# Exchanging rotation halves from POOL's queue instead of SyncE's, in a two-block model on one core

## The chip, the core and the metric

The kernel runs on one core of a Trainium2 chip. The core has TensorE (PE, matrix products), VectorE (DVE), ScalarE (ACT), GpSimd (POOL) and SyncE (SP), which here does nothing but issue transfers, and 16 DMA engines that carry them. Each engine works through its own instructions in order, and semaphores tie the engines to each other. The metric is the device time of one execution in microseconds. Lower is better.

## What is computed

256 tokens of width 1024 pass through two layers of a first block and one layer of a second. A layer of the first block projects the normalised input with one wide matrix and feeds three branches: a gated memory (mLSTM), a gated linear recurrence (RG-LRU) and a sparse attention, whose indexer keeps 64 keys for each query. A gated sum, an output projection and a feed-forward part follow. The second block has a state-space branch, a short convolution and a mixture of experts. The change touches only the rotary embedding of the attention's query, key and indexer projections:

```python
def apply_rope(x, cos, sin):
    x1, x2 = jnp.split(x.astype(jnp.float32), 2, axis=-1)
    c = cos[:, :, None, :]
    s = sin[:, :, None, :]
    return jnp.concatenate([x1 * c - x2 * s, x2 * c + x1 * s], axis=-1).astype(x.dtype)
...
        q_c = apply_rope(a_q.reshape(a_shape), cos, sin)
        k_c = apply_rope(a_k.reshape(a_shape), cos, sin)
        qi = apply_rope(a_qi.reshape(B, S, IDX_HEADS, IDX_DIM), cos, sin)
        ki = apply_rope(a_ki[:, :, None, :], cos, sin)[:, :, 0, :]
        y_c = dsa_attention(q_c, k_c, a_v.reshape(a_shape), qi, ki, a_w).reshape(B, S, D_BRANCH)
```

## The kernel before

All programs are written out by hand, one for each engine, with an explicit wait before each instruction that needs one. Features lie on partitions and tokens along the free dimension. A layer of the first block streams weight chunks of 1 MB through three slots. SP loads chunk c into `w_raw`. ACT rounds it to `w_hi` (`split`, L744), and DVE subtracts to get `w_lo` (L1256). PE then makes three products for each pair of tiles (L2118 to L2120). SP may load chunk c when the `w_lo` of chunk c - 3 is done. After each chunk every engine runs its `side(L, c)`: the small work that is placed beside the chunks.

Chunks 4 to 9 are the projections that get rotated: two each for the indexer's queries (`qi`), the queries and the keys. Call these tiles, and their pairs of buffers, 0 to 5. A tile holds two blocks of 128 features (four heads of 64) for 256 tokens:
- ACT copies PE's result out of the bank into `rope_in[n % 2]` (L804). From the third tile on it first waits until the buffer's cosine product (`rope_cos`) and exchange (`rope_swap`) are done.
- The rotation needs the upper 32 rows of a head in the place of the lower 32, and the other way round. Engines work along partitions, so transfers inside the on-chip memory do that: `swap_pair` issues four for a tile, each of 32 partitions by 512 numbers (64 KB), into `rope_sin[i % 2]`. `swap_key` issues two for the single key of the indexer. From tile 2 on `swap_pair` waits for `rope_done`, since the buffer it writes must have been used up.
- POOL multiplies `rope_in` by the cosines (L702), once for each tile.
- DVE multiplies `rope_sin` by the sines (L1356), waits for the cosine product, and adds (L1360): `rope(L, i)`. After tile 0 it rotates the indexer's key as well (L1365 to L1369).

PE computes indexer scores from `qi` and `ki` after chunks 8, 9 and 10 (L2252). The first needs three rotations: tiles 0 and 1 and the key. ACT applies the relu to them (L941), DVE sums (L1412) and selects the keys (L1428, L1430). The attention logits follow on DVE (L1454) with the row maximum (L1460), the exponential and the normalisation on ACT (L838, L849), and on PE the transposes of the probabilities after chunk 17 (L2263).

SP's part of a layer is one list. The exchanges stand in it between loads: the key's and tile 0's just ahead of load 10, tile i's ahead of load 10 + i. POOL has little to do: six cosine products, eight sums of the merge (L710), and some set-up.

Of the kernel before, what the change touches and what calls it, by code (L numbers as in the profile page):

```python
# [56 lines left out]
RING = 3  # L57
# [95 lines left out]


MERGE = max(WB)


SWAP_AT = 4 + 2 * RING

# [43 lines left out]
def program(nc, xT, positions, par_1, consts, w_in, w_a, w_x, w_branch, w_out, ffn_up, ffn_down,  # L206
            par_2, mask_2, metaT, w_in_2, w_out_2, w_group, w_expert, e_gate, e_up, e_down, out):
    ctx = ExitStack()
    with ctx:
# [221 lines left out]
        def need(eng, name, L, k):  # L431

            v = L * COUNT[name] + k
            if not isinstance(v, int) or v > 0:
                eng.wait_ge(sem[name], v)
# [83 lines left out]
        def _(sp):  # L519
# [84 lines left out]
                sp.dma_start(raw_m[i % RAWS].rearrange("p (t c) -> p t c", t=2), src)\  # L604
                    .then_inc(sem[moe_landed(i)], 16)

            def swap_halves(dst, src, first_rows, name):

                for r in first_rows:
                    sp.dma_start(dst[r:r + 32], src[r + 32:r + 64]).then_inc(sem[name], 16)  # L610
                    sp.dma_start(dst[r + 32:r + 64], src[r:r + 32]).then_inc(sem[name], 16)

            def swap_key(L):
                need(sp, "rows_ready", L, 1)
                swap_halves(ki_sin, rope_ki, (64,), "ki_swap")

            def swap_pair(L, i):

                need(sp, "evac_act", L, 2 + i + 1)
                if i >= 2:  # L620
                    need(sp, "rope_done", L, i if i > 2 else 1)
                swap_halves(rope_sin[i % 2], rope_in[i % 2], (0, 64), f"rope_swap{i % 2}")

            def layer(L, next_source):

                load(L, 2, source(L, 2))
                sp.wait_ge(sem["zeros_ready"], 1)
                load_small(L)
                for c in range(RING, MIX):
                    if c == SWAP_AT:  # L630
                        swap_key(L)
                    if SWAP_AT <= c < SWAP_AT + 6:
                        swap_pair(L, c - SWAP_AT)
                    load(L, c, source(L, c))
                load(L, MIX, ffn_source(L, 0, 0))
                load(L, MIX + 1, ffn_source(L, 1, 0))
                if L == DEPTH - 1:

                    need(sp, "y_lo", L, 5)
                    for dst, src in ((p2[:], par_2), (mask2[:], mask_2),  # L640
                                     (meta[:], metaT.rearrange("(k p) t -> p k t", p=P)),
                                     (w_route[:, :, 0:4], w_group[0].rearrange("(k p) n -> p k n", p=P)),
                                     (w_route[:, :, 4:20], w_expert[0].rearrange("(k p) n -> p k n", p=P)),
                                     (dt_w[:], w_in_2[0][:, COL_2["dt"]:COL_2["dt"] + HEADS_S]
                                      .rearrange("(k p) n -> p k n", p=P))):
                        sp.dma_start(dst, src).then_inc(sem["par_2"], 16)
                    for upper, j in ((0, 0), (0, 1), (1, 0), (1, 1)):
                        sp.dma_start(nff_m[64 * upper:64 * upper + 64, j::2],
                                     par_2[j::2, Q_NFF + upper:Q_NFF + KT:2],
                                     allow_slow_non_contiguous=True).then_inc(sem["par_2"], 16)  # L650
                with sp.Fori(0, N_FF - 1) as n:
                    load(L, MIX + 2, ffn_source(L, 0, n + 1), n)
                    load(L, MIX + 3, ffn_source(L, 1, n + 1), n)
                    load(L, MIX + 4, ffn_source(L, 2, n), n)
                load(L, PER_LAYER - 1, ffn_source(L, 2, N_FF - 1))
                load(L, PER_LAYER, next_source(0))
                load(L, PER_LAYER + 1, next_source(1))
# [24 lines left out]
        @block.gpsimd  # L682
        def _(pool):
            own = Own(pool, "own_pool")
            own(nc.gpsimd.memset(wa[:], 0.0))
            own(nc.gpsimd.memset(wx[:], 0.0))
            own(nc.gpsimd.memset(small_raw, 0.0))
            own(nc.gpsimd.memset(eps[:], EPS))
            own.settle()
            nc.gpsimd.memset(ones[:], 1.0).then_inc(sem["zeros_ready"], 1)  # L690

            def layer(L):

                for c in range(MIX - 1):
                    if 4 <= c <= 9:

                        i = c - 4
                        dst = (qi, q_c, k_c)[i // 2][:, 2 * (i % 2):2 * (i % 2) + 2, :]
                        need(pool, "evac_act", L, 2 + i + 1)
                        if i == 0:  # L700
                            need(pool, "act_lo", L, 4)
                        nc.gpsimd.tensor_tensor(dst, rope_in[i % 2], cos_t[:].unsqueeze(1).to_broadcast([P, 2, T]),  # L702
                                                ALU.mult).then_inc(sem["rope_cos"], 1)
                    if c in WB[2:]:

                        for half in range(2):
                            i = 2 * WB[2:].index(c) + half
                            b = 2 * (i % 4)
                            need(pool, "evac_dve", L, evacuations(c, True) + half + 1)
                            nc.gpsimd.tensor_tensor(merged[:, b:b + 2, :], merged[:, b:b + 2, :], merge_t[half],  # L710
                                                    ALU.add).then_inc(sem["wb_sum"], 1)

            pool.wait_ge(sem["setup_act"], 2)
            for L in range(DEPTH):
                layer(L)


            pool.wait_ge(sem["par_2"], 160)
            pool.wait_ge(sem["x_ready"], DEPTH * 8)
            nc.gpsimd.tensor_copy(hx[:, :, 0:META], meta[:]).then_inc(sem["meta_ready"], 1)  # L720
            nc.gpsimd.tensor_tensor(w_route[:], w_route[:], p2[:, Q_NFF:Q_NFF + KT].unsqueeze(2)
                                    .to_broadcast([P, KT, 20]), ALU.mult).then_inc(sem["moe_consts"], 1)

            mixed_out(pool)
            nc.gpsimd.tensor_scalar(diag[:], ident[0:20, 0:20], p2[0:20, Q_RB:Q_RB + 1], None, ALU.mult)\
                .then_inc(sem["moe_consts"], 1)
            nc.gpsimd.tensor_scalar(tri[:], cst[:, K_CAUS:K_CAUS + P], 0.0, None, ALU.is_equal)\
                .then_inc(sem["moe_consts"], 1)
            nc.gpsimd.iota(first_of[:], [[P, PER_GROUP]], base=0, channel_multiplier=0,
                           allow_small_or_imprecise_dtypes=True).then_inc(sem["moe_consts"], 1)  # L730
            nc.gpsimd.iota(place[:], [[1, SLOTS]], base=0, channel_multiplier=0,
                           allow_small_or_imprecise_dtypes=True).then_inc(sem["moe_consts"], 1)
# [2045 lines left out]
```

## Time and profile before

| | |
|---|---|
| median of 3 runs | 1684.63 us (1683.84 to 1685.64) |
| the profiled execution's own time | 1684.37 us |
| its span | 1682.4 us |
| PE busy | 1586.4 us, 94% |
| DVE busy | 1283.9 us, 76% |
| ACT busy | 946.7 us, 56% |
| POOL busy | 49.1 us, 3%, in 43 instructions |
| transfers | 325.89 MB |

The busy shares are means over a long program. The exchanges take place in two short stretches, from about 58 to 108 us in the first layer and from about 571 to 622 us in the second. The time of the profiled execution is 2.0 us longer than its span: what lies around the program. Every transfer of the kernel is issued on SP's queue, and the row of an issue tells how long SP was held by it, not how long the data took.

### The profile page before, as it was taken

The page shows a single profiled execution, that of the slowest core. Times are in us where ns is not written, and L with a number is a line of the kernel's source. Part 1 is how long each engine was busy: PE and PEld are TensorE (multiplying, and loading weights), DVE is VectorE, ACT ScalarE, POOL GpSimd, SP SyncE. Part 2 cuts the span into 40 slices and gives each one's busy share as a digit, 9 for nine tenths or more (in the row PEclk, how much of TensorE's full clock was granted, in tenths as well). Part 3 has the DMA queues.
Part 4 walks back from the last instruction along what each step waited for, and adds up shares of the span by engine and source line. Part 5 has one row for each costly group of instructions (what it writes and reads, how often), then busy time and mean ns, then how long its engine had stood idle before and what let it go on. Part 6 is the DMA issues. An engine that isn't in the chain of part 4 may idle for free.

```text
span 1682.4 us, 27823 instructions
## 1 busy us (share of the span) xinstructions
PE 1586.4 (94%) x11504; PEld 1486.7 (88%) x11504; DVE 1283.9 (76%) x1573; ACT 946.7 (56%) x1012; POOL 49.1 (3%) x43
## 2 busy tenths in 40 slices
PE   3999999999997999999999998799999899999998
PEld 3989999999997989999999997698899688888886
DVE  6798685776676798776676667885895788888986
ACT  4747655554444747655554444555643667777674
POOL 0110001000000010001000000000000000000000
PEclk9999999999998999999999999899999899999999
DMA  7455445455555465545555555254344499999993
GB/s 208 141 175 171 149 132 176 151 200 177 184 177 149 134 194 156 158 125 170 169 199 176 178 185 161 76 161 140 101 153 150 157 346 365 365 350 359 355 359 115
DMA packets 223262, 325.89 MB, mean 194 GB/s; under 512 B 21568, under 2 KB 180032, under 8 KB 223168
## 3 DMA queue, kind: packets, MB, share of 16 engines
q1 hardware_dynamic: 223168, 324.55, 58.4%
q8 instruction: 70, 1.15, 0.3%
q14 instruction: 24, 0.20, 0.0%
HBM read 320.20 MB, written 1.05 MB: 191 GB/s over the span
## 4 chain that ended last, share of the span: by engine, by line
PE 78%; DVE 13%; ACT 5%; issue 3%; DMA 1%; POOL 0%; SPq 0%; DVEq 0%; ACTq 0%
PE bank L2118 24%; PE bank L2120 23%; PE bank L2119 23%; DVE w_lo L1256 2%; ACT w_hi L744 1%; DMA w_raw<-in_w_in 1%; PE bank L2452 1%; DVE w_lo L1707 1%; DVE work L1736 1%; PE bank L2558 1%; DVE work L1250 1%; DVE work L1356 1%; PE bank L2611 0%; DVE work L1412 0%; ACT work L838 0%
## 5 line engine op out<-in xcount | busy, mean ns | idle before, releaser
L1256 DVE TENSOR_TENSOR w_lo<-w_raw,w_hi 128x2048 fp32r<-128x2048 f32 x158 | 362.8, 2296 | 121.3 <-ACT w_hi L744 120.6
L2118 PE MATMUL bank<-act_h,w_hi 128*128 128x256 f32 (+1 forms) x1408 | 406.4, 289 | 21.0 <-DVE act_l L1292 9.5
L2119 PE MATMUL bank<-act_l,w_hi 128*128 128x256 f32 (+1 forms) x1408 | 398.9, 283 | 0.0
L2120 PE MATMUL bank<-act_h,w_lo 128*128 128x256 f32 (+1 forms) x1408 | 398.9, 283 | 0.0
L744 ACT CAST w_hi<-w_raw 128x2048 fp32r<-128x2048 f32 x158 | 300.6, 1902 | 42.4 <-PE bank L2120 34.2
L2118 PEld LDWEIGHTS bank<-act_h,w_hi 128*128 128x128 f32 x1408 | 268.0, 190 | 28.0 <-issue 23.0
L2119 PEld LDWEIGHTS bank<-act_l,w_hi 128*128 128x128 f32 x1408 | 268.1, 190 | 0.4
L2120 PEld LDWEIGHTS bank<-act_h,w_lo 128*128 128x128 f32 x1408 | 267.9, 190 | 0.0
L2118 PE MATMUL bank<-u_h,w_hi 128*128 128x256 f32 x768 | 217.5, 283 | 0.0
L2120 PE MATMUL bank<-u_h,w_lo 128*128 128x256 f32 x768 | 217.2, 283 | 0.0
L2119 PE MATMUL bank<-u_l,w_hi 128*128 128x256 f32 x768 | 215.3, 280 | 0.0
L2118 PE MATMUL bank<-y_h,w_hi 128*128 128x256 f32 x704 | 200.0, 284 | 3.0 <-DVE y_l L1618 3.0
L2120 PE MATMUL bank<-y_h,w_lo 128*128 128x256 f32 x704 | 198.4, 282 | 0.0
L2119 PE MATMUL bank<-y_l,w_hi 128*128 128x256 f32 x704 | 197.5, 280 | 0.0
L2119 PEld LDWEIGHTS bank<-u_l,w_hi 128*128 128x128 f32 x768 | 146.0, 190 | 0.1
L2118 PEld LDWEIGHTS bank<-u_h,w_hi 128*128 128x128 f32 x768 | 144.1, 188 | 0.1
L2120 PEld LDWEIGHTS bank<-u_h,w_lo 128*128 128x128 f32 x768 | 143.7, 187 | 0.0
L2118 PEld LDWEIGHTS bank<-y_h,w_hi 128*128 128x128 f32 x704 | 132.2, 188 | 3.6 <-issue 3.4
L2119 PEld LDWEIGHTS bank<-y_l,w_hi 128*128 128x128 f32 x704 | 133.2, 189 | 0.2
L2120 PEld LDWEIGHTS bank<-y_h,w_lo 128*128 128x128 f32 x704 | 132.0, 188 | 0.0
L1912 DVE TENSOR_TENSOR w_lo<-w_raw,w_hi 128x2048 fp32r<-128x2048 f32 x52 | 118.8, 2289 | 13.9 <-ACT w_hi L1133 13.0
L1133 ACT CAST w_hi<-w_raw 128x2048 fp32r<-128x2048 f32 x52 | 99.3, 1912 | 36.4 <-PE bank L2120 36.4
(467 smaller groups left out, 2845.6 us busy)
## 6 DMA issues: line engine op xcount, KB each, us to landing
w_raw<-in_w_in SPq DMA_DIRECT2D x88, 1024.0 KB, 5.5
w_raw<-in_ffn_up SPq DMA_DIRECT2D x48, 1024.0 KB, 5.2
w_raw<-in_e_gate SPq DMA_DIRECT2D x25, 1024.0 KB, 7.3
w_raw<-in_ffn_down SPq DMA_DIRECT2D x24, 1024.0 KB, 4.9
w_raw<-in_e_up SPq DMA_DIRECT2D x22, 1024.0 KB, 7.1
w_raw<-in_e_down SPq DMA_DIRECT2D x22, 1024.0 KB, 7.2
w_raw<-in_w_out SPq DMA_DIRECT2D x16, 1024.0 KB, 5.0
w_raw<-in_w_branch SPq DMA_DIRECT2D x12, 1024.0 KB, 5.1
```

The source lines that it names most:

```text
L744: nc.scalar.copy(w_hi[c % RING][:], w_raw[c % RING][:]).then_inc(sem["hi_ready"], 1)
L1133: nc.scalar.copy(hi_m[i % SPLITS], raw_m[i % RAWS]).then_inc(sem["hi_ready"], 1)
L1250: step(STT(t_c, t_c, 1.0 / k, t_b, ALU.add, ALU.mult))
L1256: V.tensor_tensor(w_lo[c % RING][:], w_raw[c % RING][:], w_hi[c % RING][:].bitcast(F32), ALU.subtract).then_inc(sem[f"lo_ready{c % RING}"], 1)
L1356: own(V.tensor_tensor(rope_sin[i % 2], rope_sin[i % 2], sin_t[:].unsqueeze(1).to_broadcast([P, 2, T]), ALU.mult))
L1707: V.tensor_tensor(w_lo[c % RING][:], w_raw[c % RING][:], w_hi[c % RING][:].bitcast(F32), ALU.subtract).then_inc(sem[f"lo_ready{c % RING}"], 1)
L1736: ins = STT(dst[:, j, s:TM], psum[(2 * c + half) % 4][:, 0:TM - s], p2[:, col:col + 1], dst[:, j, s:TM], ALU.mult, ALU.add)
L1912: V.tensor_tensor(lo_m[h], raw_m[i % RAWS], hi_m[h].bitcast(F32), ALU.subtract)\
L2118: mm(out, a_hi, b_hi, start=first, stop=False, skip_group_check=True)
L2119: mm(out, a_hi, b_lo, start=False, stop=False, skip_group_check=True)
L2120: return mm(out, a_lo, b_hi, start=False, stop=last, skip_group_check=True)
L2452: ins = mm(psum[6 + g % 2][r:r + 64, o + t_0:o + T], xdt[0:rows, s, h * 64:h * 64 + 64], weight[h % 2][0:rows, col:col + n], start=s == 0, ...
```

## The change

The functions `swap_halves`, `swap_key` and `swap_pair` move from the program of SP to that of POOL, with their waits. POOL calls `swap_pair(L, i)` right ahead of the cosine product of tile i, and `swap_key(L)` ahead of that for tile 0. SP keeps its loads, and the constant that placed the exchanges among them goes. The buffers, the semaphores and the transfers themselves stay as they are.

```diff
-SWAP_AT = 4 + 2 * RING
...
                 for c in range(RING, MIX):
-                    if c == SWAP_AT:
-                        swap_key(L)
-                    if SWAP_AT <= c < SWAP_AT + 6:
-                        swap_pair(L, c - SWAP_AT)
                     load(L, c, source(L, c))
...
+            def swap_halves(dst, src, first_rows, name):
+
+                for r in first_rows:
+                    nc.gpsimd.dma_start(dst[r:r + 32], src[r + 32:r + 64]).then_inc(sem[name], 16)
+                    nc.gpsimd.dma_start(dst[r + 32:r + 64], src[r:r + 32]).then_inc(sem[name], 16)
+
+            def swap_key(L):
+                need(pool, "rows_ready", L, 1)
+                swap_halves(ki_sin, rope_ki, (64,), "ki_swap")
+
+            def swap_pair(L, i):
+
+                need(pool, "evac_act", L, 2 + i + 1)
+                if i >= 2:
+                    need(pool, "rope_done", L, i if i > 2 else 1)
+                swap_halves(rope_sin[i % 2], rope_in[i % 2], (0, 64), f"rope_swap{i % 2}")
+
...
                         i = c - 4
+                        if i == 0:
+                            swap_key(L)
+                        swap_pair(L, i)
                         dst = (qi, q_c, k_c)[i // 2][:, 2 * (i % 2):2 * (i % 2) + 2, :]
                         need(pool, "evac_act", L, 2 + i + 1)
```

POOL's queue before, from the end of the set-up through the first layer's merge (L702 is the cosine product, the ISA ahead of it POOL's configuration, L710 the merge; `work` is the tensor that holds `rope_in`, `rope_sin` and the rotated tiles):

```order
L690 MEMSET ones 128x256 [waits own_pool]
L702 ISA
L702 TENSOR_TENSOR work<-work,cos_t 128x512 [waits act_lo,evac_act,setup_act]
L702 TENSOR_TENSOR work<-work,cos_t 128x512 [waits evac_act] x5
L710 TENSOR_TENSOR work<-work 128x512 [waits evac_dve] x8
```

The same place in the changed kernel, after the two issues for the indexer's key: tiles 0 and 1 whole, and the first transfer of tile 2 (lines 670 and 671 are the two issues in `swap_halves`, L697 is the cosine product):

```order
L670 DMA work<-work 32x512 [waits evac_act]
L671 DMA work<-work 32x512
L670 DMA work<-work 32x512
L671 DMA work<-work 32x512
L697 ISA
L697 TENSOR_TENSOR work<-work,cos_t 128x512 [waits act_lo,evac_act]
L670 DMA work<-work 32x512 [waits evac_act]
L671 DMA work<-work 32x512
L670 DMA work<-work 32x512
L671 DMA work<-work 32x512
L697 TENSOR_TENSOR work<-work,cos_t 128x512 [waits evac_act]
L670 DMA work<-work 32x512 [waits rope_done,evac_act]
```

Each cosine product stands behind four issues now, from the third tile on behind a wait for `rope_done` as well, and the configuration stands behind the first six issues.

SP's queue before, from the load of chunk 10 to tile 2's first transfer (L555 is a load, L610 and L611 are the exchanges):

```order
L555 DMA w_raw1<-in_w_in 128x8x256 [waits lo_ready1]
L610 DMA work<-work 32x512 [waits evac_act]
L611 DMA work<-work 32x512
L610 DMA work<-work 32x512
L611 DMA work<-work 32x512
L555 DMA w_raw2<-in_w_in 128x8x256 [waits lo_ready2]
L610 DMA work<-work 32x512 [waits rope_done,evac_act]
```

and from the load of chunk 9 in the changed kernel (L551 is the load):

```order
L551 DMA w_raw0<-in_w_in 128x8x256 [waits lo_ready0]
L551 DMA w_raw1<-in_w_in 128x8x256 [waits lo_ready1]
L551 DMA w_raw2<-in_w_in 128x8x256 [waits lo_ready2]
L551 DMA w_raw0<-in_w_in 128x8x256 [waits lo_ready0]
L551 DMA w_raw1<-in_w_in 128x8x256 [waits lo_ready1]
```

SP's loads follow each other with nothing but their own waits between them.

## Rows read from the trace of the kernel before

**Rows 1.** Waits of PE: who waited for whom, us in total, times, longest.

```profile
PE bank L2263 <- ACT work L849: 5.5, 2, 3.3
...
PE bank L2252 <- ACT work_b L941: 4.3, 2, 2.1
...
PE bank L2252 <- DVE work L1360: 2.8, 2, 1.4
```

**Rows 2.** Chain of waits, first layer: start us, us, engine and line.

```profile
56.92 0.47 ACT work L906
...
137.51 2.30 DVE tiny L1460
...
155.17 1.62 PE bank L2263 x8
```

**Rows 3.** Stretches: from:to, length, then busy us (instructions) of PE, PEld, DVE, ACT, POOL.

```profile
64.40:142.20 77.80, 74.28 (x608) 71.71 (x607) 75.43 (x119) 42.12 (x52) 11.59 (x6) 0.98 0.54 156
142.20:155.20 13.00, 9.72 (x84) 9.52 (x82) 8.94 (x29) 12.96 (x24) 0.00 (x0) 1.00 0.53 163
```

**Rows 4.** L702's summary (ns min/median/max), then timeline of POOL: start us, us, instruction.

```profile
L702 POOL TENSOR_TENSOR work<-work,cos_t x12: 1307/1632/3216, 66.8 to 611.2; 128x512 f32<-128x512 f32 x12
L702 POOLq MODIFY_POOL_CONFIG  x2: 11/11/11, 3.0 to 3.0; - x2
...
66.75 1.31 POOL L702 TENSOR_TENSOR work<-work,cos_t 128x512 f32<-128x512 f32 x1 [63.75 <-ACT work L804]
73.40 2.33 POOL L702 TENSOR_TENSOR work<-work,cos_t 128x512 f32<-128x512 f32 x1 [5.34 <-ACT work L804]
...
90.30 3.22 POOL L702 TENSOR_TENSOR work<-work,cos_t 128x512 f32<-128x512 f32 x1 [5.19 <-ACT work L804]
```

**Rows 5.** Timeline of DVE, first layer.

```profile
66.46 0.41 DVE L1246 TENSOR_TENSOR work<-work 4x256 f32<-4x256 f32 x1
66.91 1.43 DVE L1247 TENSOR_TENSOR work<-work 4x256 f32<-4x256 f32 x1
...
83.24 0.69 DVE L1360 TENSOR_TENSOR work<-work 128x512 f32<-128x512 f32 x1
...
86.22 0.29 DVE L1369 COPY work<-work 64x256 f32<-64x256 f32 x1
...
88.75 0.68 DVE L1356 TENSOR_TENSOR work<-work,sin_t 128x512 f32<-128x512 f32 x1
...
90.08 2.29 DVE L1256 TENSOR_TENSOR w_lo<-w_raw,w_hi 128x2048 fp32r<-128x2048 f32 x1
92.28 1.79 DVE L1356 TENSOR_TENSOR work<-work,sin_t 128x512 f32<-128x512 f32 x1
94.10 0.69 DVE L1360 TENSOR_TENSOR work<-work 128x512 f32<-128x512 f32 x1
...
102.71 0.68 DVE L1356 TENSOR_TENSOR work<-work,sin_t 128x512 f32<-128x512 f32 x1
...
108.60 0.69 DVE L1356 TENSOR_TENSOR work<-work,sin_t 128x512 f32<-128x512 f32 x1
...
114.22 0.69 DVE L1356 TENSOR_TENSOR work<-work,sin_t 128x512 f32<-128x512 f32 x1
```

**Rows 6.** Issues of L610 (ns min/median/max), their landing, and SP's waits, 57 to 115.

```profile
L610 SPq DMA_DIRECT2D work<-work x26: 507/590/607, 59.2 to 618.7; - x26
...
DMA to landing us min/median/max: 2.0/4.1/5.4
...
SPq L555 <- DVE w_lo L1256: 30.5, 7, 5.5
```

**Rows 7.** Timeline of ACT, first layer; in brackets its idle time before and who ended it.

```profile
77.81 0.57 ACT L804 COPY work<-bank 128x512 f32<-128x512 f32 x1
...
89.64 0.58 ACT L804 COPY work<-bank 128x512 f32<-128x512 f32 x1 [4.26 <-DMA work<-work]
...
140.04 0.51 ACT L838 ACTIVATE work<-work,tiny 128x256 f32<-128x256 f32 x1 [0.95 <-DVE tiny L1461]
```

More of the change, by code:

```diff
@@ L605, in load_moe @@
                     .then_inc(sem[moe_landed(i)], 16)
[L607 to L622, printed above, removed]
             def layer(L, next_source):
```

## Prediction

> **What bounds the kernel now.** I read first who waits on TensorE, since PE is busy for 94% of the span. Near the exchanges it waits three times in each of the two layers: 1.4 us for a rotation (DVE, L1360), 2.1 us for a relu (ACT, L941), and 2.2 to 3.3 us, some 50 us later, for the softmax's normalisation (ACT, L849) [rows 1]. Then I read the chain of waits through the first layer. From 56.9 us it runs on ACT and then on DVE, passes the rotations, reaches the row maximum at 137.5 and comes back to PE only at 155.2, with the transposes of the probabilities [rows 2]. So what PE loses at 90 and at 106 us is not paid by the end. Without those two stalls it would stand before the transposes that much earlier, and wait there that much longer. What counts is DVE's work in that stretch. The stretch view says how full DVE is: busy 75.43 of 77.80 us, with nearly all the rest in gaps of hundredths between dependent instructions [rows 3]. After it ACT is busy for 12.96 of 13.00 us. The second layer repeats the first 513 us later.
>
> The second thing to see is what POOL's cosine product costs DVE. It runs six times a layer, 1.31 us at the least [rows 4]. The first starts at 66.75, and the 4x256 product L1247 that DVE begins under it takes 1.43 us, where the same form just before took 0.41: 1.0 us lost. The fifth starts at 90.30, under a w_lo subtraction that runs to 92.4, and is stretched to 3.22 us. DVE's next product, L1356, then takes 1.79 us where it elsewhere takes 0.68: 1.1 us lost [rows 4, 5]. So a cosine product costs DVE about 1.0 us wherever both have two-input work, and it waits for the DVE instruction that was there first.
>
> **What is removed: SP's issues.** SP issues 52 exchanges, 26 a layer, at 0.59 us [rows 6]. They hold up no weight load: of the seven loads between 57 and 115 us each is released by a w_lo subtraction of DVE, for which SP waits 30.5 us in all. So a freer SP issues no load earlier. The other gain would be faster landing, since on SP an exchange stands behind a 1 MB load and lands in a median of 4.1 us. It is late only once: the fifth evacuation on ACT waits 4.26 us for a transfer and runs at 89.64, after PE had finished that chunk [rows 7]. Neither PE nor DVE waits for that evacuation. Gain: 0.
>
> **What is added: 52 issues on POOL.** No row shows a transfer issued by POOL. Call the time that one holds POOL d. From below the nearest row is SP's shortest issue, 0.51 us; from above, POOL held until the transfer lands, 4.1 us [rows 6]. Between these lie SP's usual issue (0.59) and POOL's own instruction on a tile of this size (1.31). I take d = 1.0, between the last two. The Trainium skill, "DMA: Bandwidth & Descriptors", table on latency, gives about 1 us to the first byte for a transfer issued by GpSimd and 0.6 for one by SP; taken as an estimate of d, it gives the same sum.
>
> **What is moved: each cosine product goes behind its pair's four issues, and behind their wait for rope_done.** This is the step to follow closely. POOL's order is four issues (4d), the cosine (1.5 us, between the shortest, 1.31, and the median, 1.63 [rows 4]), then the next pair. Pairs 0 and 1 start when ACT has evacuated their tiles, 0.1 us before their cosines of now (66.75 and 73.40). Pairs 2 to 5 can't begin until an earlier rotation on DVE is done: pair 2 after rotation 0 (83.9), pair 3 after rotation 1 (90.2), pair 4 after rotation 2 (94.8), pair 5 after rotation 3 (104.1). DVE wants pair i for rotation i, at 82.5 (the L1356 just before L1360), 88.75, 92.28, 102.71, 108.60 and 114.22 [rows 5]. With d = 1.0, and 2 us from the last issue to landing (the fastest landing on SP), the first layer becomes:
> pair 0: from 66.6, cosine ends 72.1, landed 72.6, wanted 82.5
> pair 1: from 73.4, cosine ends 78.9, landed 79.4, wanted 88.75
> pair 2: from 83.9, cosine ends 89.4, landed 89.9, wanted 92.28
> pair 3: from 90.2, cosine ends 95.7, landed 96.2, wanted 102.71
> pair 4: from 95.7, cosine ends 101.2, landed 101.7, wanted 108.60
> pair 5: from 104.1, cosine ends 109.6, landed 110.1, wanted 114.22
> Nothing is late; the closest is pair 2, with 2.4 us to spare. Landing at SP's median of 4.1 us instead would bring pair 2 to 92.0, still in time. The evacuation at 89.64 moves to about 89.9. For which d does the cover end? Pair 2 is late when 83.9 + 4d + 2 passes 92.28, at d = 1.6; the queue as a whole when pairs 2 to 5 follow each other without a break, 83.9 + 4(4d + 1.5) + 0.5 = 114.2, at d = 1.5. So up to 1.5 us the issues are hidden behind DVE.
>
> **Collisions.** The six cosines move by 4 to 11 us, but all still fall between 70 and 110 us, where DVE's work is two-input almost throughout. So 6 x 1.0 us are lost as before: change 0, and perhaps one more or one less. What differs is the order. By the end of rotation 1 three cosines have met DVE and not four, so PE's 1.4 us stall should shrink; as said, that is handed on to the wait at the transposes.
>
> **A program step that moves too.** The order shows POOL's configuration instruction (ISA) just ahead of the first cosine, now behind the first six issues, while before it was over at 3.0 us, long before it was needed; its own row has 11 ns [rows 4]. If its effect has a latency, the first cosine pays it. The first layer has 82.5 - 72.1 = 10 us of room there, and the evacuation at 77.81, which needs the first cosine, 5.7 us [rows 7]. Cost 0. The Trainium skill, "GPSIMD Engine Reference", section 2 (Architecture), says that the first call of freshly loaded code pays about 6 us; by that the first cosine would end at 78.1, and pair 1 at about 84, still ahead of rotation 1 at 88.75.
>
> **The sum.** Profiled execution 1684.37 us (its span 1682.4 and 2.0 around it), median of the runs 1684.63. SP's relief 0, hidden issues 0, collisions 0 (plus or minus 1.0 a layer), and 0.4 us a layer for a few small slips (the evacuation, an interfering DVE instruction): 1684.6 + 0.8 = **1685.4 us**. About 0.2%, 3.4 us, is what a measurement of this kernel can tell from no change.
>
> **Rivals.** *POOL becomes the bound of the rotations (slower).* The mechanism is d over 1.5. At d = 2.0 pair 0 ends at 76.1, pair 1 at 85.6, and pair 2, begun at once, at 95.1 with the landing at 95.6, so rotation 2 is 3.3 us late. Pair 4 lands at 114.6, against rotation 4 at 111.9: 2.7 more. Pair 5 lands at 124.1, against 120.2: 3.9 more. That is 9.9 us a layer on a full DVE, 1704 us. At 1.75 it is about half, 1694. For it: six queue steps in series with nothing in them idle. Against it: SP does the same for 0.59, and the room per pair is 2 to 8 us. At the far end, 4.1, a pair takes 17.9 us and six of them end near 174, some 60 us a layer late: 1804. Chance 0.2.
> *Descriptors and DVE get in each other's way (slower).* The rows show POOL and DVE excluding each other in two-input work. If POOL's issues also hold up DVE's copies and scalar operations, two of these a layer fall under them (the copy at 86.22 [rows 5] is one), up to one d each: 4 x 1.0 = 4 us, 1688.6. The Trainium skill, "SBUF — State Buffer", section "SBUF: two separate sides", has this rule, as the "DVE blocks DMA" trap: a transfer issued by GpSimd needs the port pair that VectorE takes for its fast copies, and which started first blocks the other; no row here has such a transfer. Chance 0.08.
> *DVE gets free (faster).* A cosine that lands on DVE's one-input or idle time costs nothing, and PE's stalls fall by 1.4 + 2.1 us. For it: 1.0 us for each cosine is real. Against: DVE is full to 142, and ACT was idle only 1.0 us before the row maximum reached it [rows 7], so an earlier DVE gains at most that until ACT binds. To pass 3.4 us both layers must gain 1.7, which takes a lower ACT cost too. 1684.6 - 2 x 1.9 = 1681. Chance 0.12.
> *The issues on POOL cost what they do on SP (no change).* With 0.59 us the pairs are ready 1.6 us sooner each, and no one waits for them: 1684.6. This lies within the forecast.
>
> **Chances.** Forecast, with that last case, 0.6; POOL bound 0.2; port 0.08; faster 0.12. The range leaves out d above about 1.8 (0.13) and gains over 3.6 us (0.06): 1681 to 1696. Faster 0.12; within 0.2% 0.62 (forecast, and a part of the port case); slower 0.26.
>
> **What would show it.** Right: POOL transfers of about 1 us, no idle time of DVE before L1356, six cosines a layer at the places above, the 1.4 us wait of PE for L1360 gone or smaller, and PE's wait for L849 longer by as much. Wrong: DVE waiting at L1356 for a transfer (d or the landing too long), its total over 64 to 142 us changed by more than 2 us (collisions), or POOL idle between its issues for long (it is the landing or the configuration, not d).

## The result, and the profile after

| | before | after |
|---|---|---|
| median of 6 runs each | 1684.82 us (1683.84 to 1686.12) | 1692.1 us (1689.82 to 1692.77) |
| profiled execution, its span | 1684.37, 1682.4 | 1692.77, 1690.7 |
| DVE busy | 1283.9 us | 1287.6 us |
| POOL busy | 49.1 us, 43 instructions | 71.0 us, 95 instructions |

The changed kernel takes 1.004 times the time of before, with a 95% interval of 1.003 to 1.005: 7.3 us slower. That is more than the 3.4 us that a measurement can tell from no change. A second set of five runs gave 1.0037 [1.0024, 1.005]. The range held the time, but the forecast was "no change", and what came is the slower side. Three executions that were far off (one of experiment 7 at 3921.8 us, two of the kernel before at 1767.0 and 8376.86) are left out of every figure. Code lines after the change are five lower than before: L1356 is now L1351, L1360 is L1355, L1256 is L1251, L849 is L844, L941 is L936.

POOL's issues first. The summaries of the first of the two issue lines, of its landing and of the cosine (ns min/median/max), and then POOL's timeline of the first layer (start us, us, instruction), to be read against [rows 4, 6]:

```profile
L670 POOL DMA_DIRECT2D work<-work x26: 496/500/727, 59.2 to 622.2; - x26
...
DMA to landing us min/median/max: 1.8/2.4/5.2
L697 POOL TENSOR_TENSOR work<-work,cos_t x12: 1277/1316/2392, 69.3 to 623.2; 128x512 f32<-128x512 f32 x12
L697 POOLq MODIFY_POOL_CONFIG  x2: 37/37/37, 69.2 to 69.2; - x2
```

```profile
68.70 0.50 POOL L671 DMA_DIRECT2D work<-work  x1
69.30 1.32 POOL L697 TENSOR_TENSOR work<-work,cos_t 128x512 f32<-128x512 f32 x1
...
92.28 0.50 POOL L671 DMA_DIRECT2D work<-work  x1
92.79 1.32 POOL L697 TENSOR_TENSOR work<-work,cos_t 128x512 f32<-128x512 f32 x1
...
107.25 0.50 POOL L671 DMA_DIRECT2D work<-work  x1
107.76 1.28 POOL L697 TENSOR_TENSOR work<-work,cos_t 128x512 f32<-128x512 f32 x1
```

An issue holds POOL for 0.50 us, half of what the sum assumed and less than the 0.59 on SP. It lands in a median of 2.4 us instead of 4.1. By every number on which the schedule rested, the change did better than forecast.

DVE's timeline of the first layer, to be read against [rows 5]:

```profile
68.02 4.67 DVE L1245 SCALAR_TENSOR_TENSOR work<-work 4x256 f32<-4x256 f32 x7
...
76.51 1.52 DVE L1378 SCALAR_TENSOR_TENSOR work<-work 4x256 f32<-4x256 f32 x1
...
82.49 0.67 DVE L1351 TENSOR_TENSOR work<-work,sin_t 128x512 f32<-128x512 f32 x1
...
87.71 1.79 DVE L1351 TENSOR_TENSOR work<-work,sin_t 128x512 f32<-128x512 f32 x1
...
92.34 2.32 DVE L1351 TENSOR_TENSOR work<-work,sin_t 128x512 f32<-128x512 f32 x1
...
96.56 3.83 DVE L1539 TENSOR_TENSOR_SCAN work<-work 128x256 f32<-128x256 f32 x4
...
107.46 3.73 DVE L1251 TENSOR_TENSOR w_lo<-w_raw,w_hi 128x2048 fp32r<-128x2048 f32 x1
```

No idle time stands before any L1351: nothing is late. But look at the durations. L1351 takes 2.32 us at 92.34, against 0.67 at 82.49. The `w_lo` subtraction takes 3.73 at 107.46, against 2.29. One instruction in each of the six places is longer than its form is elsewhere, by 1.57, 1.10, 1.11, 1.64, 1.39 and 1.44 us: 8.2 us for six cosines. The six of before cost 0.9 to 1.1 each and 6.1 together. Two of the six have kept that price: their cosines waited for a DVE instruction that was there first (their rows last 1.79 and 2.39 us where the others last 1.3). The other four cost 1.4 to 1.6 us. And L1351 at 92.34 begins while POOL is still issuing, 0.45 us before the cosine's shown start.

The stretch view (length, then busy us of PE, PEld, DVE, ACT, POOL; clock, DMA share, GB/s), against [rows 3]:

```profile
64.70:144.70 80.00, 75.94 (x621) 73.47 (x621) 77.61 (x119) 42.13 (x52) 21.45 (x30) 0.98 0.52 152
144.70:157.70 13.00, 8.16 (x70) 7.95 (x69) 8.94 (x29) 12.96 (x24) 0.00 (x0) 0.97 0.53 161
```

DVE does the same 119 instructions in 77.61 us instead of 75.43, and the stretch is 2.2 us longer. ACT's part behind it is as it was. From here on I measure "DVE's stretch" from the start of the reciprocal (L1245 before) to the start of the row maximum (L1460 before), in both layers, where DVE stands idle for hundredths only: 72.82 and 72.87 us before, 74.98 and 74.62 after. That is 3.9 us of the 8.3 between the spans.

PE's waits and its granted clock show where more went. PE's waits of after (us in total, times, longest), against [rows 1], and then the windows behind the second layer's transposes of the probabilities, after and before, each with its columns as above:

```profile
PE bank L2258 <- ACT work L844: 9.8, 2, 4.9
...
PE bank L2247 <- ACT work_b L936: 6.1, 2, 3.1
...
PE bank L2247 <- DVE work L1355: 1.8, 2, 1.1
```

```profile
673.00:676.00 3.00, 2.85 (x14) 2.85 (x15) 2.75 (x17) 3.00 (x5) 0.00 (x0) 0.50 0.22 35
676.00:679.00 3.00, 3.00 (x16) 3.00 (x16) 2.82 (x12) 0.74 (x2) 0.00 (x0) 0.50 0.81 314
679.00:683.00 4.00, 4.00 (x35) 4.00 (x35) 3.05 (x3) 0.28 (x1) 0.00 (x0) 0.97 0.00 0
```

```profile
668.00:671.00 3.00, 2.44 (x21) 2.44 (x22) 2.81 (x13) 3.00 (x5) 0.00 (x0) 1.00 0.09 10
671.00:675.00 4.00, 4.00 (x36) 4.00 (x35) 3.76 (x16) 1.17 (x3) 0.00 (x0) 1.00 0.66 255
```

After the change PE works at the lower level (0.50 of full speed, 1.2 GHz) for 6 us behind its 4.9 us wait, 16 matmuls in 3 us. Before, the wait was 2.2 us and the clock stayed at the full 2.4 GHz. PE's timeline gives the price: from these transposes to the next group of them it takes 6.59 us before (668.56 to 675.15) and 9.37 after (673.15 to 682.52).

```profile
668.56 1.09 PE L2263 MATMUL bank<-cst,work 128*128 128x128 f32 x8 [2.22 <-ACT work L849]
```

```profile
673.15 1.97 PE L2258 MATMUL bank<-cst,work 128*128 128x128 f32 x8 [4.91 <-ACT work L844]
```

So the 8.3 us between the two spans are, in order of time: 0.34 ahead of the first stretch, 2.16 in it, 0.36 up to the second, 1.75 in it, 2.78 of clock behind it, and 0.9 in the rest. The three small ones (1.6 us together) have no cause that I found.

### The profile page after: what moved, and what is told of

Its sections match the earlier page's. It is cut to its first block, busy times and chain, and to the rows that moved or that the text cites. A ratio compares the mean times of both kernels' runs of the same rounds, so it can differ in the third digit from the quotient of the medians.

```text
span 1690.7 us, 27824 instructions
## 1 busy us (share of the span) xinstructions
PE 1589.4 (94%) x11504; PEld 1489.9 (88%) x11504; DVE 1287.6 (76%) x1573; ACT 946.9 (56%) x1012; POOL 71.0 (4%) x95
## 3 DMA queue, kind: packets, MB, share of 16 engines
HBM read 320.20 MB, written 1.05 MB: 190 GB/s over the span
## 4 chain that ended last, share of the span: by engine, by line
PE 76%; DVE 15%; ACT 4%; issue 3%; DMA 1%; POOL 0%; SPq 0%; DVEq 0%; ACTq 0%
PE bank L2113 23%; PE bank L2115 23%; PE bank L2114 23%; DVE w_lo L1251 3%; ACT w_hi L739 1%; DVE work L1407 1%; DVE work L1351 1%; PE bank L2447 1%; DMA w_raw<-in_w_in 1%; DVE work L1245 1%; DVE w_lo L1702 1%; PE bank L2553 1%; DVE work L1731 1%; PE bank L2606 0%; DVE work L1539 0%
## 5 line engine op out<-in xcount | busy, mean ns | idle before, releaser
L1251 DVE TENSOR_TENSOR w_lo<-w_raw,w_hi 128x2048 fp32r<-128x2048 f32 x158 | 365.6, 2314 | 122.4 <-ACT w_hi L739 121.6
```

The costliest lines, as they stand in the source:

```text
L1251: V.tensor_tensor(w_lo[c % RING][:], w_raw[c % RING][:], w_hi[c % RING][:].bitcast(F32), ALU.subtract).then_inc(sem[f"lo_ready{c % RING}"], 1)
```

## The experiments

The first question was why a cosine product costs DVE more. Theory A: it is a lock. POOL's cosine reads two operands, and DVE's two-input work needs the same interface. The cosine now follows an issue with no wait of its own that is still open, and takes the interface while POOL is still busy issuing. Theory B: it is position. The cosines start at other moments, and meet longer DVE instructions. Theory C: POOL's transfers themselves disturb DVE. Each ratio is to runs of the kernel before that were taken together with the experiment: their median is 1685.6 us for experiments 1, 2, 4 and 5, 1684.33 for 3, 6, 7 and 8, and 1685.77 for 9.

### 1. The cosine product ahead of the issues

```diff
                         i = c - 4
-                        if i == 0:
-                            swap_key(L)
-                        swap_pair(L, i)
...
                         nc.gpsimd.tensor_tensor(dst, rope_in[i % 2], cos_t[:].unsqueeze(1).to_broadcast([P, 2, T]),
                                                 ALU.mult).then_inc(sem["rope_cos"], 1)
+                        if i == 0:
+                            swap_key(L)
+                        swap_pair(L, i)
```

> POOL issues the exchanges, but each cosine product stands ahead of its pair's four issues and not behind them. Lock theory (a cosine product that follows an issue with no wait of its own holds DVE off already during the last issue, so that DVE loses 1.4 to 1.65 us where it lost 1.0): here each cosine product is released by a semaphore again, the six cost DVE about 1.0 us each as before the change (6.1 us a layer, not 8.3), time 1685 +- 1. Rival (POOL's issues themselves hold up DVE): the loss stays, time 1690 or more.

Measured: 1687.67 us, ratio 1.001 [1.0001, 1.0018], between what I expected (1685) and the rival's 1690. DVE's stretch is 73.55 and 73.62 us: 0.7 more than before, where the changed kernel has 2.16 and 1.75 more. It is only half a test, as the timeline of POOL shows: three cosines come after idle time, and the later three, shown here, stand right behind the issues of the previous tile.

```profile
87.79 2.38 POOL L694 TENSOR_TENSOR work<-work,cos_t 128x512 f32<-128x512 f32 x1
94.01 1.31 POOL L694 TENSOR_TENSOR work<-work,cos_t 128x512 f32<-128x512 f32 x1
99.19 1.53 POOL L694 TENSOR_TENSOR work<-work,cos_t 128x512 f32<-128x512 f32 x1
```

```profile
93.56 2.32 DVE L1351 TENSOR_TENSOR work<-work,sin_t 128x512 f32<-128x512 f32 x1
```

One of the three, that of 94.01, finds a DVE instruction that began 0.45 us before it, and that one loses 1.6 us. The others cost 0.9 to 1.1.

### 2. The cosine waits until its own exchange has landed

```diff
                             need(pool, "act_lo", L, 4)
+                        need(pool, f"rope_swap{i % 2}", L, 64 * (i // 2 + 1))
                         nc.gpsimd.tensor_tensor(dst, rope_in[i % 2], ...
```

> The changed kernel, with one wait more: POOL's cosine product waits until its pair's exchange has landed, so it still stands behind the issues, and later than in the changed kernel, but it is released by a semaphore. Lock theory: 1.0 to 1.1 us of DVE for each cosine product, DVE's total back to that of before, time 1685 to 1687, more only if ACT's evacuations come late by the 2 us that the cosine waits longer. Position rival (what costs is that the cosines meet other DVE instructions now): 1690 or more, since the positions stay late. Issue rival (POOL's issues disturb DVE): 1690 or more as well.

Measured: 1685.68 us, ratio 1.0001 [0.9992, 1.0011]. One wait, which makes POOL do its work later, removes all but 0.2 us of the loss in a stretch. DVE's stretch is 72.96 and 73.09, and DVE is busy for 1284.0 us, as before. POOL's and DVE's timelines at one place:

```profile
85.31 0.50 POOL L671 DMA_DIRECT2D work<-work  x1
87.67 1.29 POOL L698 TENSOR_TENSOR work<-work,cos_t 128x512 f32<-128x512 f32 x1 [1.87 <-DMA work<-work]
```

```profile
67.98 3.09 DVE L1246 SCALAR_TENSOR_TENSOR work<-work 4x256 f32<-4x256 f32 x7
...
86.97 0.69 DVE L1352 TENSOR_TENSOR work<-work,sin_t 128x512 f32<-128x512 f32 x1
87.69 1.82 DVE L1356 TENSOR_TENSOR work<-work 128x512 f32<-128x512 f32 x1
```

L1356 begins with the cosine and loses 1.1 us, the price of before; L1352, ahead of it, is untouched. So are the seven L1246, which end at 71.07, across the start of the first cosine at 70.70: 3.09 us, where after the change they took 4.67. This speaks for A and against C, since the issues are all still there. B is not out yet: the cosines have moved too.

### 3. The kernel before, with that same wait

SP issues the exchanges as before; only the wait of experiment 2 is added on POOL. It moves the cosines of the first layer to 72.35, 83.99, 89.58, 95.68, 100.32 and 109.85, each with its idle time ahead.

> The kernel before, with SP issuing, where POOL's cosine product waits until its pair's exchange has landed. So the cosine products move to about the places of the changed kernel, but nothing is issued by POOL and each is released by a semaphore. Lock theory: 1.0 to 1.1 us each, as before, time 1685 to 1686. Position rival: slower, 1688 or more, since the cosine products meet other DVE instructions.

Measured: 1686.1 us, ratio 1.0006 [0.9998, 1.0015], DVE's stretch 72.91 and 73.12. Six other positions, and each still costs 1.0 to 1.1 us. With that theory B falls: a cosine that was released from an open wait costs the same at every place tried.

### 4. Cosine products on DVE, exchanges on SP

```diff
-        rope_in = [at(4, 2, T), at(6, 2, T)]
+        rope_in = [at(4, 2, T), at(6, 2, T), at(57, 2, T), at(59, 2, T), at(61, 2, T), at(63, 2, T)]
...
+                own(V.tensor_tensor(dst, rope_in[i], cos_t[:].unsqueeze(1).to_broadcast([P, 2, T]), ALU.mult))
                 own(V.tensor_tensor(rope_sin[i % 2], rope_sin[i % 2],
...
-                need(dve, "rope_cos", L, i + 1)
```

POOL's cosine product is gone, and the DVE products stand in `rope(L, i)`. Each tile has its own `rope_in`, so ACT no longer waits for a buffer, only for the last rotation before it writes `mv` there.

> The kernel before, with the six cosine products on DVE instead of POOL, and six buffers for the evacuated tiles so that ACT need not wait for them. POOL reads nothing in this stretch. Each product should take DVE 0.69 us where the collision took 1.0: 6 x 0.3 = 2 us a layer less on the path, time about 1681. Rival (DVE's total does not set the end here): 1685.

Measured: 1682.76 us, ratio 0.9982 [0.9973, 0.9991], between the 1681 that I expected and the rival's 1685. With experiment 5, from which the intervals can't tell it, it is the fastest kernel here. DVE's stretch is 70.31 and 70.38 us. The arithmetic closes: 72.82, less 6.1 us of collisions, plus six products of 0.6 us, is 70.3. POOL's "free" product of 1.3 us cost DVE 1.0, and DVE does the same itself for 0.6.

The gain at the end is smaller than 2 x 2.5 us. PE's windows in the second layer show what took it:

```profile
665.00:668.00 3.00, 2.86 (x14) 2.86 (x15) 2.75 (x17) 3.00 (x5) 0.00 (x0) 0.50 0.16 50
668.00:671.00 3.00, 3.00 (x19) 3.00 (x19) 2.82 (x12) 0.74 (x2) 0.00 (x0) 0.64 0.78 300
```

PE lost its stalls at the rotations and stands 5.1 us before the transposes instead. In the second layer these come 3.4 us earlier than before (665.14 against 668.56), but the next group only 1.1 us (674.04 against 675.15). The lower clock took 2.3 us back.

### 5. Cosine products on DVE, exchanges on POOL

As experiment 4, with the issues on POOL as in the changed kernel.

> As the last one, but with the exchanges issued by POOL. Nothing is left on POOL that reads in this stretch, only the issues. Lock theory: the same time as with SP's issues, within 1 us (about 1681). Issue rival (the issues themselves hold up DVE): slower than that by 1 to 2 us a layer, and DVE instructions stretched under issues.

Measured: 1683.19 us, ratio 0.9986 [0.9977, 0.9995], DVE's stretch 70.39 and 70.45 us, within 0.1 of experiment 4. All 52 issues are there, at 0.50 us, beside two-input and one-input work of DVE, and cost it no more than that 0.1. Theory C falls: the issues alone don't make the loss. In these runs it came only where a reading POOL instruction with no open wait stood behind issues.

### 6. A short instruction between the last issue and the cosine

```diff
+                        own.settle()
+                        own(nc.gpsimd.memset(tiny[:, 858:896], 0.0))
                         nc.gpsimd.tensor_tensor(dst, rope_in[i % 2], ...
```

> The changed kernel with a small POOL memset (38 columns, about 0.1 us, reads nothing) between a pair's last issue and its cosine product. If it is only the issue that the cosine product can overtake (its reading parts of POOL are idle while a transfer is issued), the memset comes between them and takes a part of the early hold away: 1686 to 1689. If the hold begins early behind any instruction without a wait, the loss stays: 1690 to 1693. POOL's own issues take 0.50 us as before in either case.

Measured: 1690.63 us, ratio 1.0035 [1.0022, 1.0048], DVE's stretch 75.28 and 75.25. Nothing is won; the pattern is that of the changed kernel. L1353 begins 0.43 us before the memset does, and is held all the same:

```profile
93.20 0.50 POOL L671 DMA_DIRECT2D work<-work  x1
93.69 0.15 POOL L698 MEMSET tiny<- 128x38 f32 x1
93.78 1.31 POOL L699 TENSOR_TENSOR work<-work,cos_t 128x512 f32<-128x512 f32 x1
```

```profile
93.26 2.39 DVE L1353 TENSOR_TENSOR work<-work,sin_t 128x512 f32<-128x512 f32 x1
```

### 7. Eight issues a tile

```diff
-                swap_halves(rope_sin[i % 2], rope_in[i % 2], (0, 64), f"rope_swap{i % 2}")
+                for b in range(2):
+                    swap_halves(rope_sin[i % 2][:, b, :], rope_in[i % 2][:, b, :], (0, 64), f"rope_swap{i % 2}")
```

The same bytes in twice as many transfers, so that a tile's issues hold POOL for 4 us, as d = 1.0 had it in the prediction.

> The changed kernel with each exchange cut in two halves, so eight issues for a pair instead of four. At 0.50 us an issue a pair takes 4.0 us, which is what the prediction worked with (d = 1.0 with four). Its schedule says that nothing comes late for DVE: the same time as the changed kernel within 1.5 us (1691 to 1693), and the early hold belongs to the last issue alone. Rival (each issue costs DVE or the path something): twice the loss of the change, about 1699.

Measured: 1691.26 us, the median of five runs of 1690.77 to 1695.69, ratio 1.0047 [1.0034, 1.0061]. Two things are in its timelines. First, no DVE instruction waits for POOL or for a transfer: the prediction's table of readiness holds at 4 us of issues a tile. Second, DVE's stretch grows to 76.97 and 75.95 us. I had expected it to stay, with the early hold bound to the last issue alone. That was wrong:

```profile
77.75 0.50 POOL L671 DMA_DIRECT2D work<-work  x1
78.26 1.32 POOL L698 TENSOR_TENSOR work<-work,cos_t 128x512 f32<-128x512 f32 x1
```

```profile
77.44 2.69 DVE L1380 TENSOR_TENSOR_SCAN work<-ones,work 4x256 f32<-4x256 f32 x1
```

The scan takes 0.68 us when undisturbed and 2.69 here, so DVE was held for at least 2.0 us. Elsewhere DVE is released about 0.1 us before the cosine's shown end, here 79.58. So the hold began at 77.45 or earlier, 0.8 us before the cosine's shown start, during the last issue but one.

The fifth cosine, whose issues follow the fourth without idle time, shows something else, in both layers:

```profile
102.21 1.70 POOL L698 TENSOR_TENSOR work<-work,cos_t 128x512 f32<-128x512 f32 x1
```

```profile
100.64 2.12 DVE L1543 TENSOR_TENSOR work<-work 128x1024 f32<-128x1024 f32 x1
102.68 3.39 DVE L1252 TENSOR_TENSOR w_lo<-w_raw,w_hi 128x2048 fp32r<-128x2048 f32 x1
```

L1543 takes 1.23 us when undisturbed and would have ended at 101.87, before the cosine's shown start at 102.21. It ends at 102.76, in the middle of the cosine's row, and then L1252 loses 1.1 us more. So this cosine took the interface twice, for 0.9 and 1.1 us, with DVE's work in between, and the first time it took it at least 0.3 us before its row begins. If L1543 was held from its own start, as the scan was, it was 1.5 us before.

### 8. The changed kernel once more

> The changed kernel once more, unedited, to see how steady its loss is and how the second layer's transposes run. Lock theory: DVE loses about 8.3 us to the six cosine products of a layer, at the same instructions as in the first trace. Clock theory for the rest of the 7 us: after the longer wait of PE before the transposes of the second layer the granted clock is 0.50 for some 6 us, where the kernel before kept 1.00; if this falls out differently from run to run, the runs spread by about 3 us. Time 1690 to 1693.

Measured: 1691.09 us, ratio 1.0037 [1.0024, 1.005], DVE's stretch 74.99 and 74.59, the same within 0.03 us. The clock was not the same: PE waited 3.6 us before the second layer's transposes and took 8.13 us to the next group, where the first trace of this kernel has 4.9 and 9.37. In the first layer, where the waits are 3.5 and 4.8 us, PE had run longer at the lower clock before it got there (a mean of 0.74 of full speed from 103 to 113 us, against 0.83). The loss on DVE is fixed; that of the clock differs between executions of one kernel. Of the 3.0 us between the two profiled times (1689.73 and 1692.77) only about 1 arises by the end of the second layer's interval. Some 2 come after 1128 us, in the second block, where the first trace has a granted clock of 0.67 over 1350 to 1355 us and this one 1.00 at the same place.

### 9. A long instruction between the last issue and the cosine

```diff
+                        own.settle()
+                        own(nc.gpsimd.memset(at(57, 4, T), 0.0))
                         nc.gpsimd.tensor_tensor(dst, rope_in[i % 2], ...
```

> The changed kernel with one POOL instruction more per tile: between the last issue and the cosine product stands a memset of 128x1024 in free memory (about 0.96 us by the set-up's row), which reads nothing; ACT waits in addition for the last rotation before it writes there. Nothing is left out. Reach theory (a reading instruction of POOL without an unmet wait takes the interface that it shares with DVE as soon as POOL's other parts are free, while the issues still run): the memset is passed as well, the hold reaches back to 1 us and more before the cosine's shown start, and DVE's stretch grows beyond the 75.0 and 74.6 us of the changed kernel, by 0.3 to 0.9 us for each cosine that finds a two-input instruction of DVE beginning in that time: 76 to 78, 1692 to 1697 us. Rival (the hold belongs to the last half microsecond before the start, whatever stands there): 75.0, 1690 to 1693. Second rival (an instruction long enough keeps the cosine apart from the issues): as with the wait, 72.8 to 73.5, 1685 to 1688.

Measured: 1693.93 us, ratio 1.0045 [1.0029, 1.0062]. DVE's stretch is 75.33 and 75.39, 0.35 and 0.8 more than in the changed kernel and less than the 76 that I had expected of the reach theory.

```profile
68.61 0.50 POOL L671 DMA_DIRECT2D work<-work  x1
69.10 0.97 POOL L698 MEMSET work_b<- 128x1024 f32 x1
70.10 1.32 POOL L699 TENSOR_TENSOR work<-work,cos_t 128x512 f32<-128x512 f32 x1
```

```profile
69.27 2.43 DVE L1248 SCALAR_TENSOR_TENSOR work<-work 4x256 f32<-4x256 f32 x2
```

Two of these take 0.86 us undisturbed, and here 2.43. The hold was therefore at least 1.57 us long and, released 0.1 us before the cosine's end, began at 69.7 or earlier, in the middle of the memset and 0.4 us before the cosine's shown start. So a full microsecond of another instruction does not keep the cosine apart from the issues, and the second rival falls. The first (the last half microsecond only) falls with the 0.8 us of experiment 7. The fifth cosine again cost DVE twice:

```profile
98.20 1.68 POOL L699 TENSOR_TENSOR work<-work,cos_t 128x512 f32<-128x512 f32 x1
```

```profile
96.49 4.53 DVE L1542 TENSOR_TENSOR_SCAN work<-work 128x256 f32<-128x256 f32 x4
```

These four scans take 2.44 us undisturbed. They lose 2.1, more than the whole row of the cosine. How far ahead the reach goes is not settled. The cosines that found DVE just beginning an instruction inside it lost 1.2 to 1.6 us, the others 1.1, which is why the sum came out lower than I had expected.

A kernel with two issues a tile, each of twice the rows, was meant to show whether the reach follows the number of issues. It gave no result, so that is open.

### The clock, from all traces together

The wait of PE before the transposes, and the time from there to the next group of them, are in the timeline of each kernel, twice:

| kernel | layer 1: wait, interval | layer 2: wait, interval |
|---|---|---|
| before | 3.27, 8.16 | 2.22, 6.59 |
| after | 4.84, 7.89 | 4.91, 9.37 |
| 1 | 2.22, 6.38 | 2.80, 8.12 |
| 2 | 2.87, 6.59 | 3.30, 8.00 |
| 3 | 3.34, 8.11 | 2.97, 6.60 |
| 4 | 5.01, 8.84 | 5.07, 8.90 |
| 5 | 5.01, 8.18 | 5.07, 8.46 |
| 6 | 3.72, 8.15 | 4.28, 8.04 |
| 7 | 3.36, 6.38 | 3.09, 6.59 |
| 8 | 3.49, 8.10 | 3.63, 8.13 |
| 9 | 3.69, 8.15 | 4.63, 9.35 |

The interval is 6.4 to 6.6 us six times, and in these six the windows show the full clock throughout. It is 7.9 to 9.4 us in the other sixteen, and in each of them the windows show about half speed for 3 to 6 us. The lower clock costs 1.3 to 2.8 us. The six stand behind waits of 2.2 to 3.4 us, but so do four of the others (2.80, 3.27, 3.30, 3.34), so the wait alone doesn't tell which it will be. The profiled execution of experiment 7 kept the full clock twice. That fits its time, 1691.26 us, no more than the changed kernel's, although DVE's two stretches are 3.3 us longer together; two of its other runs took 1695 us, and no trace shows their clock.

## Why the prediction was right or wrong

**What bounds the kernel.** Right. DVE's stretch decides when the transposes come: it grew by 2.16 us in the first layer, and they came 2.5 us later, of which 0.3 was there before it began.

**d = 1.0.** Measured 0.50 (the key's first 0.73). The direction was safe and the choice too high: the nearest row was SP's shortest issue, 0.51. The Trainium skill, "DMA: Bandwidth & Descriptors", table on latency, would have given the same 1 us. Its figure is for the first byte, and the row shows that POOL is free again earlier. The rival *POOL becomes the bound* (0.2) was given more than it deserved, and experiment 7 shows that even at 4 us a tile nothing is late.

**Landing, and SP's relief.** Right. Landing got faster (2.4 us), and it gained nothing: the fifth evacuation still waits 4.19 us for a transfer and runs at 89.91, since tile 2's issues begin only at 84.44, after rotation 0.

**The configuration step.** Right, at 0. It took 37 ns at 69.2 and the cosine began at 69.30. The 6 us that the Trainium skill, "GPSIMD Engine Reference", section 2 (Architecture), gives to the first call of freshly loaded code did not appear here.

**PE's stalls.** The wait for L1360 did shrink, from 2.8 to 1.8 us in total, and the wait at the transposes grew, but by 4.3 us in total and not by as much as the other fell. The late DVE is in it, and the clock too, since in experiment 8, with the same DVE, it grew by 1.6 (5.5 to 7.1). The wait for the relu (L941 before, L936 after), which the prediction left as it was, grew from 4.3 to 6.1 us.

**Collisions: the step that failed.** "So 6 x 1.0 us are lost as before: change 0." The count was right, six of six. The price was taken from cosines that had idle time of POOL ahead of them, and carried to cosines that stand right behind issues. Measured: 8.2 us instead of 6.1 in the first layer. The test that I had named for it, DVE's total changed by more than 2 us, came out just over its line (2.18). What should have warned is in [rows 4] itself: all three cosines there carry a bracket, idle time ended by ACT. The prediction said that the price held "wherever both have two-input work", and never that each had been released from a wait. What the runs put in its place: a cosine that was just released costs DVE 0.9 to 1.1 us (before, experiments 2 and 3). One behind issues costs 1.05 to 1.65 with four of them, up to 1.7 with a short memset between, up to 2.0 with eight, and 2.1 once a layer with a long memset between.

That the pair of engines exclude each other agrees with the Trainium skill, "SBUF — State Buffer", section "Who interferes with whom": a DVE instruction with two inputs in this memory and a GpSimd instruction that reads it share one read interface, and who starts first keeps it for the whole instruction. What the runs add is when an instruction starts: not where its row does.

**The range.** It held 1692.1, but by luck. It reached to 1696 for an issue time up to about 1.8 us, and the issue time was 0.50. What made the kernel slower, the price of a collision and the clock, had no share in it.

**The port rival.** It had the right sign and the wrong mechanism. It said that POOL's issues hold up DVE's copies. Issues and copies do meet, but for very little. After the change the copy at 85.18 keeps its 0.29 us, and the issue above it takes 0.59 where its like take 0.50:

```profile
84.97 0.59 POOL L671 DMA_DIRECT2D work<-work  x1
```

```profile
85.18 0.29 DVE L1364 COPY work<-work 64x256 f32<-64x256 f32 x1
```

In experiment 5 the issue keeps its 0.50 and the copy takes 0.36. Both hold in both layers. So the "DVE blocks DMA" trap, which the prediction cites, is there in both directions, at 0.07 to 0.09 us for each meeting and not at up to 1.0 us.

**The missing term.** The prediction passed each stall of PE on to the transposes as if waiting were free there. It has a price, the clock, and the trace of before shows it: the first layer's interval is 8.16 us behind a wait of 3.27, the second's 6.59 behind 2.22. It makes 2.8 of the 8.3 us between the spans. In experiment 8 the second layer's interval is 1.5 us longer than that of before. It also means that *DVE gets free* could hardly pay: experiment 4 does free DVE by 2.5 us a layer, 5 us in all, and gets 2.8.

**The sum.** 1684.6 + 0.8 against 1692.1. The missing 6.7 us are, by the profiled executions, 3.9 on DVE and the clock (1.5 to 2.8); the small slips, 0.8 in the sum, came to 1.6. These parts don't add up to the microsecond, since two executions of one kernel differ by up to 3 us.

**Shown and only argued.** Shown: the issues make no such loss without a reading instruction behind them (experiment 5), that instruction makes none behind an open wait (2), nor does a new position (3), and the hold begins before the reading instruction's shown start, across a memset and across issues (6, 7, 9). Not tested: a cosine with no open wait behind some other POOL instruction and no issue. So no run tells whether it must be issues that stand ahead. Why is only argued. The Trainium skill, "GPSIMD Engine Reference", section 4 (When to use GPSIMD), says that a transfer issued through GpSimd is worked on by a pair of its cores. The others would be idle meanwhile and could begin the next instruction, unless a wait stops all of them. That fits each run: the cosine that took the interface twice would be the free cores first and the pair afterwards. It fits the met waits too: the cosine of the changed kernel does carry a wait for the evacuation, but it was met before the issues began. No run here looks inside POOL, so this stays open, as does the length of the reach.

## What to carry to other kernels

The price of an operation on a shared interface depends on what stands ahead of it in its own queue. When a trace shows such a price, read the bracket ahead of the row too, and carry the price only to places that have the same one. Where POOL issues transfers and also computes beside a full DVE, let the computing instruction wait for something real behind the issues (here: that its transfer has landed), or give the product to DVE if DVE does it for less than the collision costs. And a stall that is "only moved" to a longer wait of PE is not free: look at the granted clock behind that wait.

## What the runs showed of the hardware

- A POOL instruction that reads took the interface from DVE up to 0.8 us before its row begins, when transfers were issued ahead of it; a 0.97 us memset in between did not prevent this, an open semaphore wait did.
- Behind eight issues, or four and a 0.97 us memset, that followed an earlier product without idle time, one product took the interface twice and cost DVE 2.0 to 2.1 us, more than its usual row of 1.3 us.
- Issuing a transfer of 32 rows of 2 KB holds POOL for 0.50 us, and the time is the same for half the bytes (0.50 in experiment 7).
- The issues by themselves cost DVE less than 0.1 us in a stretch of 70 us (experiment 5 against 4), and that is the copy under an issue, 0.36 us for 0.29. In the changed kernel the issue over the copy was the longer one, 0.59 us for 0.50.
- Between one execution and another of the same kernel, with DVE's work equal within 0.03 us, the way of TensorE's clock behind one wait made 1.2 us of difference (9.37 and 8.13).
